# Two transformer blocks on one core: rows kept in place at the ends of the down projections, old rows loaded four ahead, and a chunk stage that begins with the last 512 tokens

## The reference, cut to what matters

```python
# end of the first block
ff = (jax.nn.silu(hn @ w_gate) * (hn @ w_up)) @ w_down      # w_down: 2816 x 1024
h = h + rms_norm(ff, ffn_post_g)
# start of the second block
h = _rmsnorm(x, norm_mix[l])
proj = h @ w_in[l]                                           # cq, ck, cv among its columns
# end of the second block, the output
x = x + (jax.nn.silu(gate) * up) @ w_down[l]
return _rmsnorm(x, final_norm)
```

## Time and profile before

| what | us |
|---|---|
| median of 3 runs (lowest, highest) | 2501.93 (2500.59, 2506.01) |
| profiled execution, its own time | 2506.52 |
| its span, first to last instruction | 2504.7 |
| PE busy | 2362.1 (94%) |
| DVE busy | 1430.2 (57%) |
| ACT busy | 961.4 (38%) |
| POOL busy | 917.0 (37%) |

### The profile page before, as it was taken

How to read it: one execution, slowest core, us unless ns; L and a number is a source line. 1 busy time by engine, 2 the same in 40 slices (tenths; PEclk the granted TensorE clock), 3 DMA queues, 4 the chain that set the end, 5 groups by cost and what they waited for, 6 DMA issues and landing times. The chain is left out here.

```text
span 2504.7 us, 30380 instructions
## 1 busy us (share of the span) xinstructions
PE 2362.1 (94%) x11502; PEld 1966.5 (79%) x11502; DVE 1430.2 (57%) x2175; ACT 961.4 (38%) x1917; POOL 917.0 (37%) x755
## 2 busy tenths in 40 slices
PE   6996989899999999989999889999989999999998
PEld 5885878778888888878988667787777888888886
DVE  4899641954544566774561566332485453556676
ACT  4124542533233244444532545222443323224443
POOL 3000103587778710042112111022148877881001
PEclk9997989999999999999999999999999999999999
DMA  5221103333323368654001000132233323336865
GB/s 147 49 59 59 35 26 120 116 97 127 105 85 126 105 228 279 224 183 110 18 18 49 26 5 18 34 118 84 60 118 97 125 87 104 112 111 229 272 222 185
DMA packets 216235, 273.74 MB, mean 109 GB/s; under 512 B 17111, under 2 KB 144824, under 8 KB 213274
## 3 DMA queue, kind: packets, MB, share of 16 engines
q1 hardware_dynamic: 198538, 208.49, 27.1%
q10 hardware_dynamic: 17552, 63.31, 6.4%
HBM read 203.17 MB, written 68.55 MB: 108 GB/s over the span
## 5 line engine op out<-in xcount | busy, mean ns | idle before, releaser
L484 PE MATMUL P<-ah,wh 128*128 128x512 f32 x1120 | 440.1, 393 | 10.3 <-DVE al L514 7.8
L486 PE MATMUL P<-ah,wl 128*128 128x512 f32 x1120 | 437.8, 391 | 0.0
L485 PE MATMUL P<-al,wh 128*128 128x512 f32 x1120 | 437.8, 391 | 0.0
L484 PE MATMUL P<-wh,ah 128*128 128x512 f32 (+2 forms) x1128 | 427.0, 379 | 3.1 <-POOL wl L455 3.1
L486 PE MATMUL P<-wh,al 128*128 128x512 f32 (+2 forms) x1128 | 424.9, 377 | 0.0
L485 PE MATMUL P<-wl,ah 128*128 128x512 f32 (+2 forms) x1128 | 424.7, 376 | 0.0
L552 POOL TENSOR_TENSOR stats<-stats,epsc 128x1 f32<-128x1 f32 x90 | 33.8, 375 | 949.1 <-ACT xn L1771 234.3
L484 PEld LDWEIGHTS P<-ah,wh 128*128 128x128 f32 x1120 | 211.6, 189 | 56.5 <-DVE al L514 5.5
L486 PEld LDWEIGHTS P<-ah,wl 128*128 128x128 f32 x1120 | 211.5, 189 | 44.3
L485 PEld LDWEIGHTS P<-al,wh 128*128 128x128 f32 x1120 | 211.7, 189 | 43.4
L484 PEld LDWEIGHTS P<-wh,ah 128*128 128x128 f32 x1128 | 213.7, 189 | 39.3 <-POOL wl L455 3.3
(11 more groups left out here) (324 smaller groups left out, 4308.9 us busy)
## 6 DMA issues: line engine op xcount, KB each, us to landing
rf<-ff_rows SPq DMA_DIRECT2D x154, 256.0 KB, 5.3
stage<-in_w_down_dram SPq DMA_DIRECT2D x110, 256.0 KB, 3.7
ff_rows<-sb ACTq DMA_DIRECT2D x22, 1024.0 KB, 5.0
stage<-in_w_gu_dram SPq DMA_DIRECT2D x44, 512.0 KB, 5.2
h<-ht ACTq DMA_DIRECT2D x32, 512.0 KB, 4.9
xr<-h SPq DMA_DIRECT2D x32, 512.0 KB, 4.8
stage<-in_w_in_dram SPq DMA_DIRECT2D x22, 512.0 KB, 4.2
stage<-in_w_gate_dram SPq DMA_DIRECT2D x22, 512.0 KB, 4.2
```

Source lines behind the costliest of these rows:

```text
L484: e.matmul(out, lh, rh, start=start, stop=False, skip_group_check=onto)
L485: e.matmul(out, lh, rl, start=False, stop=False, skip_group_check=onto)
L486: return e.matmul(out, ll, rh, start=False, stop=stop, skip_group_check=onto)
```

## The change

- `DownPass`: rows stay in `CR[t]` for the residual and the norm, and `HT` is no longer written. Its two buffers hold old rows beside `XR`, so that four old rows are loaded in `start_loads` and each further load waits for the row four places earlier.
- In the second block, tiles 0 to 3: the old row is added before the last sum. `last_sum` then adds the PSUM bank to the second half of the row, which signals the row complete. ScalarE squares the first half early (`first_square_act`), and only the second half behind the last sum.
- `down_pe`: the turns of tiles 4 to 7 stand one ahead of each S4 tile; that of tile 0 is no longer there.
- The orders on ScalarE, VectorE, GpSimd and SP in this end are written anew. The low parts of the weights `c` to `c+3` are made by VectorE. SP's loads of old rows, weights and (second block) stores are interleaved.
- Chunk stage: cq and ck groups of tiles 4 to 7 come first, then those of tiles 0 to 3. The turn of tile 0 stands behind the first group, tile 1 behind the second, tiles 2 and 3 behind the third. The PSUM banks are laid out anew, and the copies of queries and keys follow all turns.

The core of the diff:

```diff
-            load_to(D + DOWN_PIECES + 1)
-            for i in range(NT):
-                if i + 2 < NT:
-                    self.ps.load(ORDER[i + 2])
-                if self.ps.new is None and i:
-                    self.ps.store(ORDER[i - 1])
+            for i, t in enumerate(ORDER):
+                if i < 4:
+                    self.ps.load(ORDER[i + 4])
+                if i in (0, 1):
+                    load_to(D + DOWN_PIECES + i)
+                if self.ps.new is None:
+                    self.ps.store(t)
             load_to(D + DOWN_PIECES + 3)
...
-            turn()
             for j in range(4):
+                turn(j)
                 for p in range(TAIL, HF):
                     ins = self.down_product(DOWN_AT["S4", p], j)
                 ins.then_inc(*mm.up((name, "S4", j)))
-                turn()
...
+        def last_sum(self, t, *ready):
+            half = CR[t][:, 512:1024]
+            for w in ready:
+                DV.wait_ge(*w)
+            DV.wait_ge(ev, (self.name, "U4" if self.g_post is not None else "x", t))
+            DV.e.tensor_tensor(half, half, P[:, t, :], ALU.add).then_inc(
+                *(ev.up((self.name, "E", t)) if self.g_post is not None else res.up((self.name, t))))
...
     def down_dve(self):     # first block
             ps.norm_dve(4)
             ps.residual_dve(6)
             ps.norm_dve(5)
             ps.residual_dve(7)
+            turn(0)
             ps.norm_dve(6)
+            end(0)
             ps.norm_dve(7)
-            turn(4, (4, 5))
-            end(0)
+            turn(1)
             end(1)
-            turn(5, (6, 7))
+            low_by_dve_to(self.down + DOWN_PIECES)
+            turn(2)
             ps.residual_dve(0)
             end(2)
-            turn(6, (4, 5))
+            turn(3)
             ps.residual_dve(1)
             ps.norm_dve(0)
             end(3)
-            turn(7, (6, 7))
+            low_by_dve_to(self.down + DOWN_PIECES + 1)
             ps.residual_dve(2)
             ps.norm_dve(1)
+            low_by_dve_to(self.down + DOWN_PIECES + 2)
             ps.residual_dve(3)
             ps.norm_dve(2)
-            turn(0, (4, 5))
             ps.norm_dve(3)
...
     def down_dve(self):     # second block, new
+                ps.residual_dve(6)
+                ps.norm_dve(4)
+                ps.residual_dve(7)
+                ps.norm_dve(5)
+                ps.residual_dve(0)
+                ps.residual_dve(1)
+                ps.norm_dve(6)
+                ps.residual_dve(2)
+                ps.norm_dve(7)
+                ps.residual_dve(3)
+                end(0)
+                end(1)
+                ps.norm_dve(0)
+                end(2)
+                ps.norm_dve(1)
+                end(3)
+                ps.norm_dve(2)
+                ps.norm_dve(3)
...
     def chunk_in_pe():
-        pair_pe("cq", c, ffn1_pass, al)
-        PE.ends("cq")
-        for th in range(2):
-            for m in range(2):
-                columns_group("ck", m, th, c + 2 + m, ck_bank(m, th), (al, ("ck", m, th)), rows_of("ffn1", th))
+        for th in (1, 0):
+            for i, (key, m) in enumerate(CHUNK_BANKS):
+                columns_group(key, m, th, first["chunk"] + i, chunk_bank(key, m, th), (al, (key, m, th)),
+                              rows_of("ffn1", th), last=0)
+                if th:
+                    for t in ffn1_pass.turns_behind[i]:
+                        ffn1_pass.turn_pe(*ffn1_pass.last_turns[t])
+            if th:
+                PE.ends("cq")
```

More of the change, by code:

```diff
@@ L1745, in residual_dve @@
             e = DV.e
[L1746 to L1756, removed]
+            x, landed = self.old_rows(t)
+            row = CR[t][:, :]
+            DV.wait_ge(landed, (self.name, t))
             if self.g_post is not None:
@@ L1767, in squares_act, with first_square_pool @@
+        def first_square_pool(self, t):
+            s, v = norm_cols(self.p, t)[0:2]
+            PL.wait_ge(zf, "eps")
+            PL.wait_ge(sq, (self.name, "m0", t))
+            PL.e.tensor_tensor(v, s, epsc[:, 0:1], ALU.add).then_inc(*rs.up((self.name, "v0", t)))
         def squares_act(self, t):
-            s = norm_cols(self.p, t)[5]
             AC.wait_ge(res, (self.name, t))
-            self.junk_free(AC, t)
-            AC.e.activation(self.xn_of(t)[:, :], HT[t % 2][:, :], ACT.Square, scale=RT, accum_out=s).then_inc(
-                *sq.up((self.name, "h", t)))
+            self.square(t, "h", slice(512 if self.new is None and t < 4 else 0, 1024), norm_cols(self.p, t)[5])
@@ L2016, in down_product @@
                 sig, key = self.DOWN_FREED[op]
-                claim(b, sig, (self.name, key, j))
+                claim(b, *((res, (self.name, j)) if (op, self.ps.new) == ("S4", None) else (sig, (self.name, key, j))))
             (h, l), (wh_, wl_, _) = self.rows_place(u), self.weight_place(u)
@@ L2150, in act, with turn @@
             ps = self.ps
+            turns = ps.early_turns
+            def turn(i):
+                if ps.new is not None:
+                    ps.turn_act(*turns[i])
             ps.sums_act(4)
@@ L2399, in down_dve, with end, turn @@
                 self.down_lower(u)
+            def end(j):
+                ps.last_sum(j, (mm, (name, "S4", j)))
+            if ps.new is None:
+                ps.residual_dve(6)
[16 more added lines that the diff above has]
+                ps.norm_dve(3)
+                return
+            def turn(i):
+                ps.turn_dve(*ps.early_turns[i])
             ps.norm_dve(4)
@@ L2403, in down_dve @@
             ps.residual_dve(7)
+            turn(0)
             ps.norm_dve(6)
+            end(0)
             ps.norm_dve(7)
-            def end(j):
-                add(("E", j), c(j, 1), c(j, 1), bank("S4", j), (mm, (name, "S4", j)), (ev, (name, "U4", j)))
-            def turn(t, banks):
-                if ps.new is not None:
-                    ps.turn_dve(t, banks)
-            turn(4, (4, 5))
-            end(0)
+            turn(1)
             end(1)
-            turn(5, (6, 7))
+            low_by_dve_to(self.down + DOWN_PIECES)
+            turn(2)
             ps.residual_dve(0)
             end(2)
-            turn(6, (4, 5))
+            turn(3)
             ps.residual_dve(1)
@@ L2499, in pool @@
             ps = self.ps
[L2500 to L2501 removed]
+            ps.sums_pool(4)
+            ps.sums_pool(5)
             ps.squares_pool(4)
@@ L2508, in pool @@
             ps.squares_pool(7)
-            low_to(self.down + DOWN_PIECES + 1)
+            if ps.new is None:
+                for t in range(4):
+                    ps.first_square_pool(t)
             ps.sums_pool(0)
```

175 lines of the change are left out of this document (99 added, 76 removed).

## The result

The changed kernel takes 2488.41 us (median of 6 runs, 2486.74 to 2492.60), the kernel before 2504.78 us in the 6 runs measured beside and ahead of it (2500.59 to 2509.49). The ratio is 0.9936, with a 95% interval from 0.9920 to 0.9951: 16.4 us, or 0.6%, faster. The forecast was 2487.0 us, faster by 14.9 us.

The account below looks back on a forecast made before the run. TensorE, busy for 94% of the span, was taken as the bound. First stretch -12.0 us and end of the program -2.9 sum to -14.9, taking the median from 2501.93 to 2487.0 us, range 2484 to 2495.

Parts of the forecast that it names:

- The bound of the first stretch: S4's first tile-by-tile matmul to first cv matmul: 66.1 us without a stall instead of 78.5; 12.0 us earlier forecast.
- First deadline: Tile 7 turned for the first cq group: VectorE ready at 1116.2, TensorE there at 1116.4, 0.2 us ahead.
- three surcharges: Added to VectorE's queue up to tile 7's low halves: 0.5 and 0.2 us for roots, 0.7 for ScalarE's high half.
- The wait of 3.29 us: VectorE at 1099.35: a wait for tile 6's old row, not GpSimd; disappears with four rows loaded ahead.
- Second deadline: Tiles 0 to 3 in the chunk stage: VectorE's turn of tile 0 ends 1134.5; TensorE loses about 0.3 us.
- The slow clock goes too: First stretch: the lower clock after long waits disappears, as no wait is left in front of it.
- Early loads at nothing: Four old rows loaded during S4: costed at 0, bounded at 2.7 us of delay for each block.
- End of the program: Last sum starts at 2494.6, last norm at 2497.3: 2.9 us earlier, bounds 4.2 and about 1.
- The wait for the root of tile 0: End of the program: VectorE, after the sums of tiles 0 and 1, waits for this root until 2491.4.
- The half square: Last row at the end of the program: only half a row squared, 0.60 us for the 1.06 of a whole.
- The starved roots: GpSimd's inverse roots find no gap on VectorE: partly 2493 us (0.17, shared with half gain), all 2506 us (0.03).

Follow-up runs that it names:

- the kernel with the second part alone: Against the kernel before: only the change at the end of the program, first block and chunk stage as before; 2501.64 us, ratio 0.9984.
- SP's order mended: Against the changed kernel: SP issues the loads of rows 0, 1 and 2 before the first store, row 3 behind one store; 2485.90 us, one run.
- The run with whole squares: Against the changed kernel: ScalarE squares whole rows behind the last sum, without the early half square; 2485.53 us, one run.
- the kernel with one more addition: Against the changed kernel: one more small GpSimd addition, result unused, some 5 us before the first that counts at the end; 2488.62 us, one run.

## Why the prediction came out right, point by point

- **The bound of the first stretch** (66.1 without a stall, 66.5 forecast) held: 66.27. The 12.0 us are 12.2. It held in the six other profiles with the whole first block and chunk stage of the change, 66.26 to 66.27.
- **First deadline.** The low halves of tile 7 start at 1109.73 and are done at 1111.0; TensorE wants them at 1111.43. The forecast left 0.2 us between them, it was 0.4. Its three surcharges were the root of tile 7 at 0.5 (0.51 at 1095.05), its second root at 0.2 (0.2: the norm at 1100.70 starts 0.79 behind a sum, where others are followed after 0.59) and ScalarE's high half of tile 6 at 0.7 (0.57 at 1105.48). The weight's low part, which no row of this stretch had priced, follows its neighbours at 1.14 (forecast 1.15).
- **The wait of 3.29 us** that the earlier trace rows put down to GpSimd was read as a wait for the old row of tile 6. The residual at 1090.80 waits for nothing. That it waited for the row fits: the root of tile 6 was done at 1094.06, and the row, issued at 1092.28, would have taken 7.1 us, inside the 4.7 to 9.3 of the earlier trace rows. That the cure is four rows ahead is not shown: with two ahead, but the row loads in front of the weights on SP, it didn't wait either. Of the two edits that came together the one that the forecast did not name is enough; four ahead behind the weights was not run. The size was right.
- **Second deadline.** 0.3 us were forecast at the turns of tiles 2 and 3. They take 1.66 us (1129.58 to 1131.24), 0.08 over two bare ones. VectorE was through with its last turn at 1133.3, and the group that needs it starts at 1131.24 + 5.46 = 1136.7.
- **The slow clock goes too**: 1.00 in every window of the stretch. What it had cost was read as one number; the kernel with the second part alone took 2.5 us more for the same stretch in its profiled execution, against which the gain is 14.7 us instead of 12.2.
- **Early loads at nothing.** TensorE is busy in all of 1060 to 1070, as before, and has no wait up to 1180. The delay was there all the same, on the rows behind the loads: ScalarE waits 4.16 us for one up to 1063.82, where before it waited 1.68 us, up to 1066.39. By the start of the first stretch that is 2.5 us later, near the 2.7 that were the bound, and ScalarE's lead swallowed it.
- **End of the program.** The forecast had the last sum 1.6 us behind the start of the last matmul (2494.6 and 2493.00) and the last norm 2.7 behind that. Measured: 1.45 and 2.79, and the store chain of 4.5 us behind (2480.40 to 2484.9), as before (2500.21 to 2504.7). 2.9 us were forecast, 3.0 came. The reason, too, is confirmed: row 1 was added 4.67 us behind its issue (2459.19 to 2463.86, 4.5 forecast), row 3 4.3 behind its own (2466.69 to 2470.99), and with SP's order mended the last sum starts on TensorE's end.
- **The wait for the root of tile 0** was forecast at about 1.5 us and is 1.20.
- **One term stood in the wrong place.** The half square was counted as gain on the last row. The run with whole squares shows it hidden there, behind the norm of tile 2; it is worth 0.6 us through the rows in front.
- **The starved roots** (0.17 and 0.03) didn't come, though VectorE's queue has hardly a gap. The roots slip in between neighbours, at 0.19 + 0.55 us or up to 2.7 for a pair, and VectorE stands for them only 0.5 and 0.9 us in the first block. At the end one was starved, 4.67 us, but it belonged to a row that nobody wanted soon. One reading of the earlier trace rows was wrong: the power at 1115.22 did not end with a VectorE instruction but at 1116.76, 0.40 us behind the end of an addition of VectorE (1115.13 and 1.23).
- **What the median did besides.** 14.9 us were forecast, 15.2 are between the marks of the two profiles, and 16.4 between the medians, whose interval (12.3 to 20.0 us) takes in both. The changed kernel measured again was 18.5 us faster (14.5 to 20.8), so the gain of the whole may be somewhat above what lies between the marks; no run settles it. That the absolute time came within 1.4 us of the forecast is partly luck: the kernel before went up from 2501.93 to 2504.78 with three more runs, and the gain came out larger by half of that. The profiled span was forecast at 2489.8 and was 2484.9; that miss is the 5.0 us that came ahead of the first mark.

## What to carry to other kernels

If TensorE waits for rows that another engine prepares, look first for work that asks for nothing new and can stand in front of the wait: here going back to the old order of groups cost 9.6 of 12.2 us in the stretch and 2.3 more behind it. Sum the preparing engine's queue up to each point where TensorE will ask for its work, with starts of neighbours as prices and a surcharge for each root or square that comes from elsewhere; in this case a margin forecast at 0.2 us was 0.4. Then ask of each queue what stands behind a waiting instruction: the two small losses that were found, 1.2 us with rows two ahead and 1.2 us at the end of the program, were loads that stood behind other transfers on SP.

## What was not expected of the hardware

- **The two engines block each other both ways.** The forecast counted only small GpSimd instructions held up by VectorE. A GpSimd subtraction of 128 x 1024, 2.38 us, that started 0.1 us ahead stretched a VectorE instruction of 1.28 us to 3.33 and 3.38. The rule of the Trainium skill (SBUF — State Buffer, section "SBUF: two separate sides"), by which the first to start keeps the shared pair for its whole instruction, agrees with these rows.
- **When a small GpSimd instruction finds its opening is not settled.** In the first block it got in between VectorE neighbours without a gap; at the end of the program it passed five such boundaries in 4.67 us. It took 4.67 in all ten profiles with the changed end, and 3.54 in both with the old one. A long pause of GpSimd is excluded as the cause. The kind of the neighbours alone is not it: in the kernel with one more addition the added one (2449.37 and 0.57) was done 0.04 us behind the end of a low half, and the next one passed a boundary between the same two lines at 2454.64. What decides it was not tried.
- **The clock behind a wait of TensorE varies.** The same wait of 2.77 us stood in a window with a mean clock of 1.00 in one execution and of 0.72 in another, and the stretch was 2.5 us longer; and the untouched first 1090 us differed by up to 5.5 us between profiles. For changes of a few us only marks on both sides of the change tell anything.
